# Memory keys and values in three passes of split operands

## The reference

```python
def memory_attention(qm, mem_n, w_mem_kv):
    ...
    kv = mem_n @ w_mem_kv
    km = kv[..., :MEM_W].reshape(B, M, N_HEADS_MEM, HEAD_DIM)
    vm = kv[..., MEM_W:].reshape(B, M, N_HEADS_MEM, HEAD_DIM)
    ...
    logits = jnp.einsum('bshd,bmhd->bhsm', q, km).astype(jnp.float32) * (HEAD_DIM ** -0.5)
    p = jax.nn.softmax(logits, axis=-1).astype(vm.dtype)
    return jnp.einsum('bhsm,bmhd->bshd', p, vm).reshape(B, S, MEM_W)
```

## Time and profile before

| | us |
|---|---|
| median of 3 runs | 1152.37 |
| lowest and highest | 1152.14, 1152.72 |
| the profiled execution, its own time | 1152.8 |
| its span, first to last instruction | 1151.0 |
| PE busy, share of the span | 1098.7 (95%) |
| POOL busy | 146.5 (13%) |

### The profile page before, as it was taken

How to read it: one execution, slowest core, us unless ns; L and a number is a source line. 1 busy time by engine, 2 the same in 40 slices (tenths; PEclk the granted TensorE clock), 3 DMA queues, 4 the chain that set the end, 5 groups by cost and what they waited for, 6 DMA issues and landing times.

```text
span 1151.0 us, 13994 instructions
## 1 busy us (share of the span) xinstructions
PE 1098.7 (95%) x5702; PEld 505.3 (44%) x5702; DVE 295.4 (26%) x662; ACT 215.4 (19%) x397; POOL 146.5 (13%) x67
## 2 busy tenths in 40 slices
PE   8999999999999999999999999999999999999996
PEld 7889999833333333333333333333333333333332
DVE  4586575431111121111111111111111111111112
ACT  5454555421000001000000010000000100000002
POOL 5862667600000000000000000000000000000000
PEclk9999999999999999999999999999999999999999
DMA  9754547999999999999999999999999999999995
GB/s 355 259 198 147 167 147 311 373 400 426 428 425 427 428 427 428 428 428 428 428 429 429 428 428 428 428 428 428 428 428 429 428 428 428 428 429 428 429 427 228
DMA packets 50257, 443.82 MB, mean 386 GB/s; under 512 B 6138, under 2 KB 9644, under 8 KB 25644
## 3 DMA queue, kind: packets, MB, share of 16 engines
q1 hardware_dynamic: 48448, 442.17, 92.1%
q10 hardware_dynamic: 1772, 1.14, 0.3%
HBM read 441.66 MB, written 1.05 MB: 385 GB/s over the span
## 4 chain that ended last, share of the span: by engine, by line
PE 67%; DMA 25%; DVE 5%; ACT 2%; issue 1%; SPq 0%; POOL 0%; DVEq 0%
PE psum L1580 27%; PE psum L1615 15%; PE psum L1254 14%; DMA my_area<-in_w_up 9%; DMA ring<-in_w_up 9%; DMA xv_area<-in_w_up 6%; PE psum L1543 4%; DVE gate_area L1182 1%; DVE gate_area L1178 1%; DVE gate_area L1176 1%; PE psum L1602 1%; ACT gate_area L829 1%; DMA mem_s<-in_mem 1%; PE psum L1589 1%; PE psum L1329 1%
## 5 line engine op out<-in xcount | busy, mean ns | idle before, releaser
L1580 PE MATMUL psum<-ring,gate_area 128*64 128x512 f32 x1344 | 304.5, 595 | 14.6 <-DMA ring<-in_w_up 14.4
L1580 PEld LDWEIGHTS psum<-ring,gate_area 128*64 128x64 f32 x1344 | 93.3, 137 | 212.4 <-issue 168.7
L823 ACT ACTIVATE gate_area<-gate_area 128x512 f32<-128x512 f32 x32 | 20.1, 630 | 751.8 <-DVE gate_area L1174 751.8
L590 POOL TENSOR_TENSOR unit_lo<-ring,unit_hi 128x1024 fp32r<-128x1024 f32 (+1 forms) x62 | 146.1, 2364 | 75.9 <-ACT unit_hi L623 75.8
L1615 PE MATMUL psum<-ring,gate_area 128*64 128x512 f32 x624 | 141.6, 594 | 4.6 <-ACT gate_area L829 4.6
L1174 DVE TENSOR_SCALAR gate_area<-psum 128x512 f32<-128x512 f32 x32 | 22.1, 692 | 461.7 <-PE psum L1589 461.7
L1185 DVE COPY pT_s<-psum 128x512 f32<-128x512 f32 x32 | 22.1, 692 | 281.5 <-PE psum L1615 281.5
L1615 PEld LDWEIGHTS psum<-ring,gate_area 128*64 128x64 f32 x624 | 44.2, 137 | 84.6 <-issue 79.6
L1580 PE MATMUL psum<-xv_area,gate_area 128*64 128x512 f32 x320 | 73.6, 595 | 6.9 <-DMA xv_area<-in_w_up 6.9
L623 ACT ACTIVATE unit_hi<-ring 128x1024 fp32r<-128x1024 f32 (+1 forms) x62 | 64.2, 1037 | 50.8 <-PE psum L1254 47.6
L1543 PE MATMUL psum<-pT_s,gate_area 64*128 64x512 f32 x264 | 65.6, 615 | 0.8 <-DVE pT_s L1185 0.8
(11 more groups left out here) (244 smaller groups left out, 1086.8 us busy)
## 6 DMA issues: line engine op xcount, KB each, us to landing
ring<-in_w_up SPq DMA_DIRECT2D x84, 2048.0 KB, 28.7
ring<-in_w_down SPq DMA_DIRECT2D x39, 2048.0 KB, 33.8
xv_area<-in_w_up SPq DMA_DIRECT2D x20, 2048.0 KB, 30.4
my_area<-in_w_up SPq DMA_DIRECT2D x16, 2048.0 KB, 30.3
pl_area<-in_w_down SPq DMA_DIRECT2D x14, 2048.0 KB, 27.3
my_area<-in_w_down SPq DMA_DIRECT2D x7, 2048.0 KB, 30.2
ring<-in_w_gate SPq DMA_DIRECT2D x6, 2048.0 KB, 8.0
ring<-in_w_in SPq DMA_DIRECT2D x4, 2048.0 KB, 14.3
```

Source lines behind the costliest of these rows:

```text
L590: nc.gpsimd.tensor_tensor(lo, src, hi.bitcast(F32), ALU.subtract).then_inc(lo_ready, 1)
L823: nc.scalar.activation(sig, glu, ACT.Sigmoid, scale=ALPHA).then_inc(sig_ready, 1)
L1580: ins = nc.tensor.matmul(psum[lo:lo + SLOTS, c, :], lhsT, w[:, at:at + 512], start=(k == 0), stop=False)
```

## The change

- The memory tokens are kept in two parts: ACT writes `memT_hi` (eight activations), DVE writes `memT_lo` from PSUM and `memT_hi` (eight instructions in place of the eight that wrote `memT`, each pair behind a wait for ACT).
- The block `KV` becomes four units, 22 to 25: two of 128 columns for the keys, and two "quads" (four chunks of 128 rows by 256 columns) for the values. The gates' units begin at 26.
- PE makes `kmT` and `vm` by `three_passes`: 96 products in place of 32. For `vm` both quads are used in turn by the two blocks of rows, so the first quad is given back after three quarters of the job.
- ACT splits units 25 to 28 among the copies of `qmT`, `kmT` and `vm`.
- The ring slot of `KV` comes free when POOL is through with unit 25.

```diff
 UNITS += [("QM", "cols", c) for c in range(2)]
+UNITS += [("KV", "cols", c) for c in range(2)] + [("KV", "quads", j) for j in range(2)]
 UNITS += [(f"G{g}", "cols", c) for g in range(6) for c in range(4)]
...
+    if name == "KV":
+        if j == 1:
+            return "bank_filled", FILLED["kmT" if kind == "cols" else "vm"]
+        return "unit_used", 5 * (KC // 2 - 1) + (2 if kind == "cols" else 3)
...
+        memT_lo = at("memT_lo", [P, KC, M], qe_at + 2 * PIECE_W, F32R)
...
+        memT_hi = at("memT_hi", [P, KC, M], memT_at, F32R)
...
+            if kind == "quads":
+                src = w[:, 4 * j:4 * j + 4, 256:512]
...
-                    if before_it in LAST_SPLIT:
-                        sp.wait_ge(lo_ready, LAST_SPLIT[before_it])
-                    else:
-                        sp.wait_ge(bank_filled, LAST_USE[before_it])
+                    sp.wait_ge(lo_ready, LAST_SPLIT[before_it])
...
-            for u in range(11, 15):
-                split(u)
+            split(11)
+            for j in range(4):
+                t = empty(("memT", j))
+                for c in range(2):
+                    k = 2 * j + c
+                    ins = nc.scalar.activation(memT_hi[:, k, :], t[:, c * M:(c + 1) * M], ACT.Copy,
+                                               scale=gT[:, KC + k:KC + k + 1])
+                ins.then_inc(memT_hi_ready, 1)
+                if j == 1:
+                    split(12)
+            split(13)
+            split(14)
...
-            act.wait_ge(bank_filled, FILLED["vm"])
+            split(25)
             copy("kmT", kmT, pair)
+            split(26)
+            split(27)
             copy("vm", vm_s, pair)
+            split(28)
...
+                dve.wait_ge(memT_hi_ready, j + 1)
                 for c in range(2):
                     k = 2 * j + c
-                    ins = nc.vector.tensor_scalar(memT[:, k, :], t[:, c * M:(c + 1) * M], gT[:, KC + k:KC + k + 1],
-                                                  None, ALU.mult)
+                    ins = nc.vector.scalar_tensor_tensor(out=memT_lo[:, k, :], in0=t[:, c * M:(c + 1) * M],
+                                                         scalar=gT[:, KC + k:KC + k + 1], in1=memT_hi[:, k, :].bitcast(F32),
+                                                         op0=ALU.mult, op1=ALU.subtract)
...
-            n = block_arrived(pe, "KV")
             pe.wait_ge(dve_emptied, EMPTIED["memT", 3])
-            w = ring_block(n, 512)
-            done(project_T(fill("kmT"), w, 0, memT, 2))
+            t = fill("kmT")
+            for c in range(2):
+                chunk_T(t[:, c * M:(c + 1) * M], c == 1, (memT_hi, memT_lo))
             t = fill("vm")
+            units = [next_unit()]
             for b in range(B):
+                s = slice(b * P, (b + 1) * P)
                 for k in range(KC):
...
+                    if b == 0 and k == 4:
+                        units.append(next_unit())
+                    hi, lo = units[k // 4]
+                    ins = three_passes(t[:, b * 256:(b + 1) * 256], (memT_hi[:, k, s], memT_lo[:, k, s]),
+                                       (hi[:, k % 4, :], lo[:, k % 4, :]), k == 0, k == KC - 1)
+                    if b == 1 and k == 3:
+                        ins.then_inc(unit_used, 1)
             done(ins)
```

More of the change, by code:

```diff
@@ L117 @@
 UNITS += [(f"O{hf}", "rows", j) for hf in range(2) for j in range(KC // 2)]
+G_UNIT = UNITS.index(("G0", "cols", 0))
 P_UNIT = UNITS.index(("P", "cols", 0))
@@ L172 @@
         EMPTIED["br", _f, _n] = _f + 1
-LAST_USE = {"KV": FILLED["vm"]}
 LAST_SPLIT = {name: n + 1 for n, (name, _, _) in enumerate(UNITS)}
@@ L186, in unit_read @@
         if j < KC // 2 - 1:
-            return "unit_used", 5 * (KC // 2 - 1) + 1 + hf * (KC // 2 - 1) + j + 1
+            return "unit_used", 5 * (KC // 2 - 1) + 3 + hf * (KC // 2 - 1) + j + 1
         return "bank_filled", FILLED["out", B - 1, hf]
@@ L379, in hybrid_layer_kernel @@
         xT_hi_ready = sem("xT_hi_ready")
+        memT_hi_ready = sem("memT_hi_ready")
         got_eps = sem("got_eps")
@@ L440, in unit_views @@
             w = ring_block(FRONT.index("PA" if name == "P" else name), cols)
-            src = w[:, 2 * j:2 * j + 2, :] if kind == "rows" else w[:, :, j * P:(j + 1) * P]
+            if kind == "quads":
+                src = w[:, 4 * j:4 * j + 4, 256:512]
+            else:
+                src = w[:, 2 * j:2 * j + 2, :] if kind == "rows" else w[:, :, j * P:(j + 1) * P]
             k, n = src.shape[1], src.shape[2]
@@ L717, in gate @@
                   .then_inc(act_emptied, 1)
-                u = 22 + m + UNIT_SLOTS
+                u = G_UNIT + m + UNIT_SLOTS
                 if u < len(UNITS):
@@ L1323, in _, with chunk_T @@
             done(ins)
[L1325 to L1333, removed]
+            def chunk_T(t, last_of_job, rhs=(xT_hi, xT_lo)):
                 hi, lo = next_unit()
                 for k in range(KC):
-                    ins = three_passes(t, (hi[:, k, :], lo[:, k, :]), (xT_hi[:, k, :], xT_lo[:, k, :]), k == 0,
+                    ins = three_passes(t, (hi[:, k, :], lo[:, k, :]), (rhs[0][:, k, :], rhs[1][:, k, :]), k == 0,
                                        k == KC - 1)
@@ L1343, in _ @@
                 chunk_T(t[:, c * S:(c + 1) * S], c == 1)
-            n = block_arrived(pe, "KV")
             pe.wait_ge(dve_emptied, EMPTIED["memT", 3])
-            w = ring_block(n, 512)
-            done(project_T(fill("kmT"), w, 0, memT, 2))
+            t = fill("kmT")
+            for c in range(2):
+                chunk_T(t[:, c * M:(c + 1) * M], c == 1, (memT_hi, memT_lo))
             t = fill("vm")
+            units = [next_unit()]
             for b in range(B):
+                s = slice(b * P, (b + 1) * P)
                 for k in range(KC):
-                    ins = nc.tensor.matmul(t[:, b * 256:(b + 1) * 256], memT[:, k, b * P:(b + 1) * P], w[:, k, 256:512],
-                                           start=(k == 0), stop=(k == KC - 1))
+                    if b == 0 and k == 4:
[5 more added lines that the diff above has]
+                        ins.then_inc(unit_used, 1)
             done(ins)
```

## The result

The changed kernel takes 1156.82 us (median of 7 runs, 1155.61 to 1157.86) against 1152.69 us of the kernel before in the same comparison (7 runs). The ratio is 1.0036, with a 95% interval of 1.0027 to 1.0045: slower by 4.1 us, or 0.36%. The profiled execution has a span of 1155.0 us, 4.0 more than before.

What follows compares the result with a forecast made beforehand. It took PE's front, then the experts' weight stream, as the bounds. Products' -2.3 us ended in a wait for DVE, held +3.6 by POOL, leaving +2.4: 1152.37 + 2.4 = 1154.8 us, range 1152.2 to 1158.2.

Steps and rivals of the forecast that it cites:

- the first rival: PE's new wait before heads 0 and 1: the clock falls in it, +4.1 to +5.8 us, likeliest 1156.5; chance 15%.
- The products: Memory keys and values on PE: 96 matmuls take 11.5 us in place of 13.82, alone -2.3 us (-1.9 to -2.4).
- the two parts of the tokens: ACT's copies and DVE's instructions at 38 to 43 us: cost nothing, at most some 0.3 us if gaps are overrun.
- The units: POOL's units 25 to 28, between 84 and 97 us: each ready in time, PE never waits for one.
- POOL on DVE: End of the second search: POOL's units 27 and 28 hold two DVE instructions, +3.6 us on DVE (3.4 to 4.0).
- Where PE waits: After gate 1 at 100.6 PE waits for softmax of head 0, then head 1, started at 105.75 instead of 103.35.
- The term of +2.4: PE's start on head 1: the wait ends 2.3 us of gain and adds 2.4 (bounds 2.2 and 2.8).
- The clock: PE's wait before head 0: clock expected at 1.00 around 105; a fall would add 1.7 us once to twice.
- The likeliest case: Both POOL units meet DVE: 1154.8 us, own range 1154.5 to 1155.2, chance 55%.
- Front and stream: PE's front and the experts' weight stream: a microsecond's shift of the front moves the stream and the end by as much.
- The second and third rival: DVE beside POOL's new units: second, one unit meets DVE, 1152.7 (10%); third, DVE not held at all, 1151.2 (12%).

Runs made afterwards that it cites:

- before_pool: The kernel before, with four subtractions of 1024 columns on POOL whose result nobody reads: 1156.19 us against 1152.81, ratio 1.0028.
- after_busy16: The changed kernel with 16 matmul calls on a constant tile put on PE just ahead of the first scores: 1155.62 us against 1152.88 of the kernel before.
- later_bias: The changed kernel with DVE's closing of the second search behind the first two softmaxes, bias parts behind the first attention output: 1150.80 us against 1152.88 of the kernel before.
- late_dve: The changed kernel with DVE's closing of the second search and bias parts moved behind the first two softmaxes: 1154.91 us against 1152.81 of the kernel before.
- late_dve_before: The kernel before, with DVE's closing of the second search and bias parts moved behind the first two softmaxes: 1156.85 us against 1152.81, ratio 1.0034.
- mix_early: The changed kernel with DVE's copy of the pooling bank put between the two searches: 1156.30 us against 1152.88 of the kernel before, ratio 1.0035.

## Why the prediction came out as it did

The direction and the range held, the range because it took in the first rival. The likeliest time, 1154.8, was 2 us short, and what came to pass was that rival, to which I had given 15%.

- **The products**: -2.3 forecast, 2.28 less in the chain. Right. So were the two parts of the tokens: DVE ended them at 43.67 (43.5 forecast), and nobody waited.
- **The units**: forecast at 84.6, 87.9, 91.75 and 94.1, seen at 84.70, 88.07, 91.90 and 94.24. PE waited for none of them.
- **POOL on DVE**: L978 forecast to end at 94.25 and L981 at 96.7, seen at 94.43 and 96.78. before_pool shows that the cause is POOL, and the maxima came at 101.55 (101.4 forecast).
- **Where PE waits**: wrong. The sentence "PE is through with gate 1 at 100.6, waits for head 0" left out that the scores themselves need a bank which DVE empties, with the very instruction that follows the held ones. I had followed `p_ready` from DVE to PE and not the banks, though the list of jobs gives them by counting eight back. The wait of 3.9 us stood ahead of the scores and not behind gate 1. For the length of the sum it made almost no difference, since the softmax was still to come at 105.8: after_busy16 has +2.45 at the mark with the clock up. The term of +2.4 came out by luck in this respect: the wait for the bank ended early enough to be hidden behind the wait for the softmax.
- **The clock**: the step that failed is the chance. The likeliest case had the clock at 1.00 through a wait of nearly 4 us; the granted clock fell to 1.2 GHz in it. The price of that (1.7 to 3.4 us on top) was about right, 1.8 to 2.0 at the mark, and a little high for the end, 1.4. Its source was weak: the slow first matmuls of the earlier trace rows were taken as a low clock, but the profile has the granted clock at 1.00 from 0 to 5 us, so these rows show double spacing and not its cause. The seven runs have mean clocks of 0.995 to 0.997 over the span where the runs of before in the later comparisons have 0.998 to 1.000. So it most likely fell in each of them, not only in the profiled one. The 2 us between them are not explained by it: two runs of 1156.51 have 0.995, one of 1157.54 has 0.996.
- **Front and stream**: +4.43 at the mark, the same 4.43 at the first matmul on the attention outputs (186.92 against 182.49), +4.0 in the span. The coupling was as described. At 260 us it is still +4.33 (DVE's L1199 at 260.07 against L1176 at 255.74); the remaining 0.3 came back among the experts, and its cause stays open.
- **The second and third rival**, that one or none of DVE's instructions is held, are refuted by the two durations. The sentence in the third that even then the full -2.3 was out of reach was true of DVE's order as it was; later_bias reaches it by another order.

## What to carry to other kernels

A piece of work that is free on an idle engine may not be free for its neighbour. Before units are added to GpSimd, list the VectorE instructions that fall into their time, and of these the kinds that were held here: TENSOR_TENSOR with two SBUF inputs, and TENSOR_SCALAR and CAST from SBUF to SBUF. Then ask for each result of VectorE that comes late who needs it: not only its data, but also the PSUM bank that it empties. And price a new wait on TensorE twice, once for its length and once for the clock behind it.

## What the runs showed of the hardware

- Of two GpSimd instructions back to back, exactly one held VectorE instruction comes through between them: in the changed kernel L978 ends at 94.43 and L981, begun at 94.46, is held by a unit that had begun at 94.24. It works the other way too: in late_dve POOL's two units take 5.04 in place of 4.73 us. The first, from 100.38, takes 2.37; the second, from 102.71, takes 2.71, and DVE's 128x768 cast, held since 100.39, ends inside it at 103.16. The Trainium skill (SBUF — State Buffer, Who interferes with whom) has it that whoever issues first keeps the port for the whole instruction; the rows agree.
- Not every VectorE instruction is held: MATCH_REPLACE8 at 92.41 takes its 0.41 us inside a unit of POOL.
- How long an idle must be for the clock to fall is not one number in these runs. It fell in a wait of 3.9 us (the changed kernel) and behind waits of 2.4 (late_dve_before) and 3.1 (mix_early), and in the profiled executions of late_dve and before_pool it held behind 3.1 and 2.2. In late_dve_before and mix_early it fell only after PE had begun to work again, in mix_early with a second wait of 0.52 in between. What decides between them stays open.
